# A two-layer block on one core: the attention values of two steps ago, moved from behind the second dense piece to ahead of this step's scores

## What is computed

```python
# tokens lie on a grid of 8 rows x 64 columns; each query sees all 8 rows and 16 columns, and the 16 meta keys
s_loc  = einsum(q / sqrt(64), k_rows) + bias          # -inf outside the 16 columns
s_meta = einsum(q / sqrt(64), k_meta)
p      = softmax(concat([s_loc, s_meta], axis=-1))
og     = einsum(p_loc, v_rows) + einsum(p_meta, v_meta)
o_na   = rmsnorm(concat(om, og)) ; mix = concat(o_na, o_gl) @ w_o
```

## Time and profile before

| | us |
|---|---|
| median of 3 runs (1452.45 to 1454.73) | 1452.77 |
| the profiled execution, device time | 1450.83 |
| its span, first to last instruction | 1449.0 |
| TensorE busy in the span | 1426.3 |
| the stage of the 18 steps | about 141 to 247 |

### The profile page before, as it was taken

The page is one execution under the profiler, slowest core; times in us unless marked ns, Lnnn a source line. Parts: engine busy times, 40 slices in busy tenths (PEclk is TensorE's granted clock), DMA queues, the critical chain, the costliest instruction groups (busy, mean ns, idle before and its releaser), DMA issues.

```text
span 1449.0 us, 21152 instructions
## 1 busy us (share of the span) xinstructions
PE 1426.3 (98%) x8888; PEld 1232.9 (85%) x8888; DVE 814.3 (56%) x1169; ACT 557.0 (38%) x880; POOL 536.2 (37%) x227
## 2 busy tenths in 40 slices
PE   9999999999999999999999999999999999999997
PEld 8988887999999999889788767678878888888887
DVE  6942655256666666446799689854463343432123
ACT  6533444453322323223523474464343332333221
POOL 2421211424443443543344323314434443545441
PEclk9999999999999999999999999999999999999999
DMA  7210220212222225876232212112223343322332
GB/s 255 88 59 30 86 72 30 88 59 88 94 96 88 95 96 204 289 259 223 72 102 92 86 59 88 59 44 96 93 74 131 102 144 118 117 100 90 107 111 87
DMA packets 44829, 154.75 MB, mean 107 GB/s; under 512 B 4992, under 2 KB 7808, under 8 KB 44736
## 3 DMA queue, kind: packets, MB, share of 16 engines
q1 hardware_dynamic: 44080, 150.79, 30.6%
q10 hardware_dynamic: 656, 2.62, 0.6%
HBM read 151.17 MB, written 2.10 MB: 106 GB/s over the span
## 4 chain that ended last, share of the span: by engine, by line
PE 88%; DVE 8%; ACT 2%; issue 2%; DMA 0%; SPq 0%; DVEq 0%; ACTq 0%
PE G L525 79%; DVE scb L2354 1%; DVE small L2352 1%; PE G L842 1%; PE B L803 1%; PE B L1128 1%; PE G L750 1%; PE B L1152 1%; PE B L1100 1%; DVE G L1827 1%; PE G L1139 0%; PE B L820 0%; DVE rstd L1857 0%; PE B L495 0%; DVE kend L1935 0%
## 5 line engine op out<-in xcount | busy, mean ns | idle before, releaser
L450 POOL TENSOR_TENSOR wlo<-raw,whi 128x1024 fp32r<-128x1024 f32 x222 | 535.7, 2416 | 889.7 <-ACT whi L1244 889.7
L1244 ACT ACTIVATE whi<-raw 128x1024 fp32r<-128x1024 f32 x224 | 236.4, 1056 | 279.7 <-DMA raw<-wstream 169.6
L525 PE MATMUL G<-xhi,whi 128*128 128x512 f32 (+1 forms) x692 | 273.5, 395 | 2.0 <-DVE xlo L1835 1.8
L525 PE MATMUL G<-xhi,wlo 128*128 128x512 f32 (+1 forms) x692 | 267.4, 386 | 0.0
L525 PE MATMUL G<-xlo,whi 128*128 128x512 f32 (+1 forms) x692 | 266.9, 386 | 0.0
L525 PE MATMUL G<-uhi,whi 128*128 128x258 f32 (+3 forms) x1200 | 257.9, 289 | 3.9 <-DVE ulo L2167 0.8
L525 PE MATMUL G<-ulo,whi 128*128 128x258 f32 (+3 forms) x1200 | 250.8, 283 | 0.0
L525 PE MATMUL G<-uhi,wlo 128*128 128x258 f32 (+3 forms) x1200 | 250.2, 282 | 0.0
L525 PEld LDWEIGHTS G<-uhi,whi 128*128 128x128 f32 x1200 | 188.9, 189 | 16.7 <-issue 13.5
L525 PEld LDWEIGHTS G<-ulo,whi 128*128 128x128 f32 x1200 | 189.2, 189 | 0.0
L525 PEld LDWEIGHTS G<-uhi,wlo 128*128 128x128 f32 x1200 | 189.0, 189 | 0.0
(11 more groups left out here) (355 smaller groups left out, 1679.0 us busy)
## 6 DMA issues: line engine op xcount, KB each, us to landing
raw<-wstream SPq DMA_DIRECT2D x225, 512.0 KB, 3.3
ada_in<-ada SPq DMA_DIRECT2D x40, 512.0 KB, 5.9
ada_late<-ada SPq DMA_DIRECT2D x8, 512.0 KB, 3.7
h<-hT SPq DMA_DIRECT2D x8, 264.0 KB, 3.2
out<-res SPq DMA_DIRECT2D x8, 256.0 KB, 2.2
biasn<-bias SPq DMA_DIRECT2D x2, 960.0 KB, 8.3
biasn<-bias ACTq DMA_DIRECT2D x2, 960.0 KB, 4.7
scan_keep<-scanm SPq DMA_DIRECT2D x1, 528.0 KB, 6.8
```

Source lines behind the costliest of these rows:

```text
L450: pool.tensor_tensor(wlo[:, i, :], raw[:, i, :], whi[:, i, :].bitcast(F32), ALU.subtract)\
L525: ins = pe.matmul(dst[:, x, 0:xw], w[:, slot, b * P:(b + 1) * P], u[:, k, off + x0:off + x0 + xw], start=(first and i == 0 and j == 0), st ...
L1244: act.activation(whi[:, m % RING, :], raw[:, m % RING, :], ACT.Copy).then_inc(s["unit_hi"], 1)
```

## The change

In steps 2 to 17 the values V(st-2) are issued first in TensorE's step, ahead of the scores S(st). The second and third piece of a step then follow each other with nothing between them. No instruction is added or removed, and the programs of the other engines and all DMAs are the same.

```diff
@@ -864,17 +864,15 @@
             values_by_token(0)
             for st in range(18):
                 ps = na_pieces(st)
+                if 2 <= st <= 17:
+                    na_values(st - 2)
                 if st < 16:
                     na_scores(st)
                 for x in ps[0:1]:
                     piece(x)
                 if 1 <= st <= 16:
                     na_transposes(st - 1)
-                for x in ps[1:2]:
-                    piece(x)
-                if 2 <= st <= 17:
-                    na_values(st - 2)
-                for x in ps[2:3]:
+                for x in ps[1:3]:
                     piece(x)
                 if st in (5, 9, 13, 17):
                     na_factors((st - 5) // 4)
```

## The result

The changed kernel takes 1459.59 us, the median of five runs (1457.87 to 1459.61), against 1452.45 for the kernel before in the same comparison: a ratio of 1.005, with a 95% interval of 1.0039 to 1.0061. Measured once more on another occasion it was 1459.29 against 1451.62, a ratio of 1.0057 (1.0044 to 1.0070). So the change makes the kernel about 7 to 8 us slower. Two executions that took far longer than all others of their kernel, 3609.56 us in e2 and 1753.83 us of the kernel before beside e1 to e4, are left out of all medians and ratios. The forecast was 1461.0, within 1456.5 to 1464.0, with 0.93 for slower.

A forecast was written before the change was run, and what follows sets the result against it. The prediction took TensorE as the bound, busy 106.55 of 111 us in the attention stage. Its step terms summed to 8.17 us, taking the median from 1452.8 to 1461.0, range 1456.5 to 1464.

The forecast's parts named there:

- Step 2: V(0) at its new place waits for VectorE's copy of T(0), less a saved switch: +1.35 us.
- Steps 4, 7, 10: Third piece begins a new tile and loses V as cover while VectorE empties it: +0.91, +0.39, +0.30 us.
- Steps 6 and 10: V(4) and V(8), opening a head pair, wait for ScalarE's copy of the factors: +1.48 us each.
- The saved switches: V no longer splits two dense pieces; 0.2 us saved each in plain three-piece steps 5, 9 and 11: -0.60.
- steps 11 and 12: Step 11 saves a switch, 0.2 us; in step 12 V(10) fills S(12)'s wait for the k tile, -0.72 us.
- The tail: Steps 13 to 17, without dense pieces: V(12) and V(13) wait for copies, S(15) starts late: +3.58 us.
- rival (d): TensorE's clock falls to 1.2 GHz in steps 14 to 17: +11 to +13 us, 1464 to 1466; chance 0.05.
- The sum of 8.17: All predicted losses and gains of the steps added, in us, lengthening the span from 1449.0 to 1457.2.
- (a): Part of the waits is hidden, by earlier copies or the loop of steps 14 to 17: +3.3, 1456; chance 0.12.
- (b): Kernel gets faster: switches saved in seven steps, step 12's wait filled, nothing waits: -2.1, 1450.7; chance 0.02.
- (c): Scores or a piece start past the waiting V on TensorE, so no change: 1452.8 us; chance 0.03.

The follow-up runs named there:

- e2: Kernel before with the values ahead of the scores in steps 14 to 17 only; 1454.78 us, ratio 1.0029.
- e1: Kernel before with the values ahead of the scores in steps 2 to 13 only; 1456.39 us, ratio 1.0035.
- e4: Changed kernel with VectorE's gated linear attention of steps 1 to 4 moved to the end of its step; 1457.65 us, ratio 1.0047.
- e8: The changed kernel itself measured again, with nothing altered; 1459.29 us, ratio 1.0057 to the kernel before.
- e6: Changed kernel with ScalarE copying the factors ahead of the values by token in steps 5, 9 and 13; 1458.67 us, ratio 1.0045.
- e5: Changed kernel with three added matmuls ahead of V(12) in step 14, filling its pause; 1459.32 us, ratio 1.005.
- e10: The changed kernel itself a third time, one run, with nothing altered; 1459.35 us.
- e3: Changed kernel with V(4), V(8) and V(12) back behind the second dense piece in steps 6, 10 and 14; 1454.37 us, ratio 1.0018.
- e7: Kernel before with V at chosen places in steps 2, 5, 9, 11, 12 and 13, elsewhere as before; 1449.72 us, ratio 0.9985.

## Why the prediction was right, point by point

The starts of the groups on TensorE, counted from S(0) in each profile, give every step's share. The V that stands newly ahead of a group (1.02 or 0.81) is taken off.

| up to | before | changed | lost so far | predicted |
|---|---|---|---|---|
| S(3) | 16.52 | 18.90 | 1.36 | 1.35 |
| S(5) | 29.31 | 32.35 | 2.23 | 2.26 |
| turning of factors, step 5 | 36.35 | 38.39 | 2.04 | 2.06 |
| S(7) | 43.11 | 47.55 | 3.42 | 3.54 |
| S(9) | 55.91 | 60.48 | 3.76 | 3.93 |
| turning of factors, step 9 | 63.67 | 67.26 | 3.59 | 3.73 |
| S(10) | 64.74 | 70.52 | 4.97 | 5.21 |
| S(11) | 72.06 | 78.36 | 5.28 | 5.51 |
| S(13) | 86.06 | 91.18 | 4.31 | 4.59 |
| turning of factors, step 17 | 105.24 | 114.20 (e8: 112.99) | 8.96 (7.75) | 8.17 |

- **Step 2.** V(0) waits 1.47 us for VectorE's copy, and S(3) has lost 1.36 by it (1.35 predicted). e4 takes the wait away by freeing VectorE's queue.
- **Steps 4, 7, 10.** The tile boundaries are where they were expected, 0.87, 0.34 and 0.31 by the table (0.91, 0.39, 0.30 predicted; step 10's is S(11) less S(10)).
- **Steps 6 and 10.** V(4) and V(8) cost 1.38 each where 1.48 was said. The release was shorter than the 0.15 us that I took from a release by VectorE. In the changed kernel ScalarE's copy of the factors ends at 181.25 + 0.57 = 181.82 and V(4) starts at 181.87, 0.05 later:

```profile
181.25 0.57 ACT L1480 ACTIVATE rbs<-G 128x512 f32<-128x512 f32 x1
```

It is 0.05 at V(8) too. That is no figure for ScalarE in general: in e6, where the small copy L1453 comes last, V(4), V(8) and V(12) start 0.10, 0.25 and 0.30 behind its end.
- **The saved switches.** Steps 5 and 9 give 0.19 and 0.17 (0.2 predicted), steps 11 and 12 together 0.97 (0.92).
- **The tail.** Without the slow clock, that is in e8, 4.27 are lost up to S(13) and the tail costs 7.75 - 4.27 = 3.48 us where 3.58 was predicted. V(13) waits 0.79 and V(14) 1.24 for VectorE's copies in e2, e4, e5, e6, e8 alike, and V(15) stays late by what VectorE's loop is late.
- **The clock, rival (d).** It had 0.05 and a price of up to 5 us for slow matmuls. Two of three profiles of the changed kernel have the clock at its 1.2 GHz level behind V(12)'s pause, at a price of 1.2 and 1.4. The stretch is short (3.4 us at 0.54 in the first profile), and there a part of the work that it slows would have waited anyway: V(13) waits 0.37 us where it waits 0.79 without the fall. In e10 it waits 0.79 all the same. So the price was mis-sized and the chance too small. That the pause brings the clock down, which is the mechanism of (d), is not shown: four other profiles with this pause (e2, e4, e6, e8) have no fall behind it, and three (e3, e5, e6) have one with no pause ahead of it, as the last section shows. The Trainium skill, "TensorE: Matmul & The Clock Gate", section "Why this matters for your kernels", warns of long gaps; in these profiles the half clock also stands in stretches without one.
- **The absolute times.** The sum of 8.17 stands for a median that moved by 7.1 and 7.7 us in the two comparisons. The measured 1459.59 lies 1.4 below the forecast: 1.0 by this difference, and 0.3 since the kernel before had 1452.45 in the comparison and not 1452.77. The single runs of one kernel spread over 1 to 5 us, so the tenths of the stage can be tested in a profile and not in a median.
- **The other rivals.** That part of the waits is hidden (a) fell to e1 and e2, that the kernel gets faster (b) to the result. That something passes a waiting V (c) was not seen: what follows V starts behind it in each of these timelines.

## What to carry to other kernels

On an engine that is the bound, moving a group forward is a question asked of each instance by itself: what does it wait for, when is that there, and what did it cover in its old place. Here the 16 instances of one line met waits of 0.8 to 1.5 us, lost covers of 0.3 to 0.9, and gains of 0.2 to 0.7; a choice for each instance turned a stage that was 8 us longer into one that was 2.4 shorter. The most expensive ones together were the first of head pairs 1 to 3: they need three copies by ScalarE that begin only when the turnings right before them are done. When the profile names one releaser of several, the others may be as late: reordering ScalarE's copies in e6 brought 0.3 and 0.4 us at two places and nothing at the third.

## What the hardware showed that I had not expected

TensorE's clock falls to its 1.2 GHz level now and then, and these profiles don't say why. With the same pause of 1.5 us ahead of V(12) it fell in two profiles of the changed kernel and stayed in a third, and in e2, e4 and e6 as well. But a pause is not needed. In e3, e5 and e6 it fell ahead of the stage, for some 3 us from about 134 or 135 us on, and TensorE was in dense matmuls without a wait when it did. The first window is e5's, the second that of the kernel before, whose profile has no fall there:

```profile
134.00:137.00 3.00, 3.00 (x15) 2.82 (x14) 1.13 (x2) 2.19 (x5) 2.38 (x1) 0.50 0.42 108
```

```profile
134.00:137.00 3.00, 2.76 (x22) 2.55 (x21) 1.36 (x3) 2.67 (x5) 2.39 (x1) 1.00 0.33 91
```

The kernel before is not free of it either, as its timed runs suggest: beside e5 to e7 the four with a mean granted clock of 0.999 took 1450.59 to 1450.76 us, and the two with 0.996 took 1453.59 and 1453.72. Where in them the clock fell is not on record. So nothing here ties the falls to the change. What draws it in one execution and not in the next stays open.

Going from dense float32r matmuls to the attention's and back costs 0.2 us together: the earlier trace rows said so before, and steps 5 and 9 of the changed kernel gave back 0.19 and 0.17.
